# A hybrid decoder step with streamed expert rows: ring of eight, three weight places, reworked first attention and new order tables

## The chip, the cores and the metric

The kernel runs on one core of a Trainium2 chip. The metric is the device time of one launch in microseconds. The kernel before took 2222.21 us (median of 3 runs, 2209.38 to 2229.83). The engines are TensorE (PE), VectorE (DVE), ScalarE (ACT), GpSimd (POOL) and SyncE (SP), and 16 DMA engines that SP's and POOL's queues feed.

## What is computed

One inference step for 256 prompt tokens (tiles A and B, 128 tokens each) and 8 sample tokens (tile S), two layers, all in float32, D = 1024. Every sub-layer is RMS-normed and modulated (shift, scale, gate) by a vector from `silu(c) @ w_mod + b_mod`. Layer 0 mixes tokens by latent attention (the samples over 2048 cached positions), layer 1 by a gated MLP (SGU) with causal 128x128 mixing. Each is followed by PEER, which fetches 16 experts for each of 8 heads of each token:

```python
q = (xt @ w_q).reshape(PEER_BLOCK, PEER_HEADS, 2, PEER_HALF)
s1 = jnp.einsum('thk,nk->thn', q[:, :, 0], sub_keys[0])
s2 = jnp.einsum('thk,nk->thn', q[:, :, 1], sub_keys[1])
t1, i1 = lax.top_k(s1, PEER_TOPK)
t2, i2 = lax.top_k(s2, PEER_TOPK)
cand = (t1[..., :, None] + t2[..., None, :])   # 16 x 16, of which again the top 16
idx = e1 * N_KEYS + e2
g = jax.nn.softmax(top, axis=-1)
act = jax.nn.gelu(jnp.einsum('thkd,td->thk', u_tab[idx], xt))
out = jnp.einsum('thk,thkd->td', g * act, v_tab[idx])
```

## The kernel before

**Tiling and stages.** `schedule()` writes the program as a list of stages, which all engines walk in the same order: init, modulation chunks (`mod`), norm, `mla_in`, `attn`, `tables` (transposed keys), `proj`, norm, then `query` and one `route` for each head; after this come tile B, the samples and their eight `cache` stages, the SGU stages of layer 1 (`sgu_v`, `sgu_u`, `sgu_mix`, `sgu_out`), and the sample chain at the end (`proj`, `query_s`, `topk_s`, 16 `sgu_s`, `sgu_out`, `query_s`, `topk_s`). An engine signals each finished piece of a stage by one semaphore count, and others wait for the count (`after`, `begin`).

**The stream.** A *slot* is one expert index of one head: a gather of 128 rows of peer_u (1024 floats each) into `uring` and one of peer_v into `vring`. There are 512 slots for the prompt and 16 for the samples. POOL issues the gathers (`gather`, L779) in the order of the string PLAN_POOL: U and V, with K and C for cache pages. It waits for the indices of the head (DVE's "topk") and, from slot 7 on, for the slot's place in the ring to be free. DVE takes a U row (`dot`, L1932), 16 dots are put through a gelu in `gelu` (P) and `weights` (W), ACT makes a scaled diagonal from each weight (`diagonal`, L1453), and PE adds the V row, times that diagonal, to `yacc` (`value_sum`, L1217). A U row's place is free after the dot, a V row's after PE. When all slots of a tile are summed, DVE copies `yacc` out (`drain`, Y).

**Order.** The stream is woven into the stages by tables. At every signal, link and point an engine calls `spot()`; PLAN_PE, PLAN_DVE and PLAN_ACT say at which count how many units of the stream follow (V on PE; U, P, W, Y on DVE; D, T on ACT). PLAN_SP says the same for weight chunks on SP.

**Weights.** They come in chunks of 0.75 to 1 MB (`load_chunk`, L673). After the first query chunk they go through `wring`, four places; before it, while the rings are unused, uring and vring give six more places (`AHEAD`). A place is loaded again when PE has used its chunk. `EARLY` puts modulation chunks 8 to 19 inside `mla_in` and `attn` of tile A: 2 and 2, then 4 and 4.

**Steps that the change touches.** `rsqrt` (L1515 to L1521) is a chain of 14 small DVE instructions, each waiting for the one before. `norm` takes its square sum on DVE (L1524), then makes h in two passes over 1024 columns. `attn` goes through two halves of four heads, one after the other, in one set of buffers. `gate_row` and `residual` copy a row block from PSUM on DVE (L1678, L1670). `pick` (L1706 to L1733) finds the experts of one head; its last signal, "topk", releases the gathers.

Of the kernel before, what the change touches and what calls it, by code (L numbers as in the profile page):

```python
# [16 lines left out]
U32 = mybir.dt.uint32  # L17
# [28 lines left out]
RING = 7  # L46
WRING = 4
# [64 lines left out]
189:VVVVVVVVVVVVVVVV 197:VVV 199:V 200:VVVVV 207:V 208:VVVVVV 213:VVV 217:VV 218:V 232:V 237:VV 239:V 260:VV 280:V  # L112
285:V 290:VV 295:V 300:VVVVVVVVV 320:VVVVVVVVVVVVVVVVVVVVVVVVVV 323:VVVVV 331:VVV 334:VVVV 339:VVVVV 342:VVVV 358:V
361:VVVVVVVV 363:VV 364:VV 369:V 379:V 382:VV 383:V 397:VVVVVVVV 399:V 400:VVVV 405:V 417:VVVVVVVVVV 422:VV 426:VVV
428:V 460:VVV 503:VVV 508:VVVV 529:VVV 534:VVVV 557:VV 565:VV 567:VVV 569:VVVVVVVVVVVVV 581:VV 582:VV 595:V
596:VVVVVVVVVV 598:V 599:V 604:VV 629:VV 631:VV 639:VVVV 640:V 650:V 654:VVVVVVVVV 656:V 657:VV 662:V
676:VVVVVVVVVVVVVVV 677:V 688:V 691:VVVVVVVVV 693:V 694:VV 699:V 703:VVVVV 707:VVV 709:V 741:VVV 784:VVV 789:VVVV
810:VVV 815:VVVV 838:VV 840:VVVVVVVVVVVVVVVVVVVVV 854:V 855:VV 869:VVVVVVVV 871:V 872:VV 877:V 902:VV 904:VV 912:VVV
913:V 919:V 923:V 927:VVVVVVVVV 929:V 930:VVV 935:V 949:VVVVVVVVVVVVVVVVVVV 950:V 964:VVVVVVVV 966:V 967:VV 972:VV
976:V 985:VV 990:VVVVV 993:VV 1000:VV 1002:VV 1004:VV 1006:VV 1008:VV 1012:V 1013:VVVV 1019:VVVVVVVVVVVVVVVVV  # L120
1025:VV 1027:V 1039:VV 1042:V 1048:V 1054:V 1060:V 1066:V 1072:V 1075:VV 1079:VVVVV 1081:V 1090:VVV 1092:V 1094:V
1102:VV 1109:V 1111:V 1113:V 1115:V 1117:V 1121:V
1122:VVVVVVVVVVVVVVVVVVVVVVVVVVVVVVVVVVVVVVVVVVVVVVVVVVVVVVVVVVVVVVVVV 1128:VVVVVV
"""
PLAN_ACT = """
121:T 127:DDDDDDDDDDDDDDDD 145:TDDDDDDDDDD 147:D 148:D 149:DDDD 158:TDDDDDDDDDD 162:DDDTDDD 173:D 179:DD 181:TDD
186:DDD 190:DDD 196:DDDD 208:DD 210:DDDDD 215:DDD 219:DDDDDDD 229:TDDDDDDDDDDDDDDDD 242:T 243:DDDDDDDDDDDDDDDD 252:T
263:T 264:D 267:DDDDDDDDDD 269:DD 270:DD 283:DD 284:D 298:TDDDDDDDDDD 300:DDDDDDDDDDTDDDDDDDDD 318:D 335:DDD 338:T
356:DDD 359:DDDDDDDDDDD 373:T 379:DD 381:DDDDD 394:DD 398:DDDDD 402:DDDD 406:DD 407:DD 408:TDD 421:D
422:DDDDDDDDDDDD 425:TDD 436:DD 438:DDDDD 447:D 448:D 458:TD 462:DDDDDDDDDD 464:DD 465:DDDDDD 470:DDTDDD 474:DDDD  # L130
482:D 483:D 494:D 497:DDDDTDDDDDD 499:DDDDDDDDDDD 507:DT 524:DDD 545:DDD 548:DDDDTDDDDDDD 568:DD 570:DDDDD 575:DD
579:DDDDDDDD 583:DDDDD 587:D 588:TD 589:DD 603:DDDDDTDDDD 605:DD 606:D 617:DD 619:DDDDD 629:D 630:T 635:D 639:DT
643:DDDDDDDDDD 645:DDD 646:DDDD 651:DDDDDDDDDD 655:DDDD 663:DD 664:D 666:T 678:DDDDDDDDD 680:DDTDDDDDDDDDD 695:DDDD
701:DDDDDDDD 708:D 709:D 713:DDDDTDDDDDDDTDDDDDDDTDDDD 722:DDDDD 739:DDDD 756:D 759:DDTDDDDDDDDDD 775:DDD 781:DDDDT
788:D 789:DDD 793:DDDDDDDDDDDTDDDDDDDDDDDDDDDDTDDDDDDDDTDDDDDDDDDDDDDDDDDDDDDDDDDD
"""
PLAN_DVE = """
210:U 224:U 252:U 266:U 287:U 301:UUUUUU 333:U 347:U 368:U 382:U 401:U 402:P 403:UW 417:U 437:U 438:U 452:U 476:U
# [28 lines left out]
VVVVVVVVVVVVVVVVVVVVVVVVVVVV  # L167
"""
PLAN_SP = """
1:WWWWWWWW 30:WWWWWWWWWWWW 34:WWWWWWWWWWWWWWWWWWWWWWWWWWWWWWWWW 124:WWWWWWWWWWWWWWWWWWWW 181:WWWWWWWW  # L170
224:WWWWWWWWWWWWWWWWWWWWWWWWWWWWWWWWWW 341:WWWWWWWWWWWW 367:WWWWWWWWWWWWWWWWWWWWWWWWWWWWWW 458:WWWWWWWWWWWWWWWW
516:WWWWWWWWWW
"""
# [1844 lines left out]
```

## Time and profile before

| what | us |
|---|---|
| median of 3 runs | 2222.21 |
| lowest, highest | 2209.38, 2229.83 |
| span of the profiled execution | 2207.0 |
| PE, DVE, POOL, ACT busy | 1531.2, 1395.3, 1212.1, 355.5 |
| first gather issued at | 163.35 |

The profiled execution is known by its span alone, from its first to its last instruction; it lies 15.2 us below the median. Busy shares are means over stages of very different kinds, so the windows (busy time of each engine in a stretch, with the granted TensorE clock as a share of 2.4 GHz, the busy share of the DMA engines, which by its counting can pass 1, and GB/s) say more than the page. In the timeline a row is one instruction, or several alike, with the time that its engine was idle before and what ended that.

### The profile page before, as it was taken

To read this page: it belongs to the slowest core of one execution; us is meant where nothing else is said; L and a number is where in the kernel's file an instruction comes from. 1 tells how busy PE (TensorE), PEld (TensorE's weight loads), DVE (VectorE), ACT (ScalarE), POOL (GpSimd) and SP (SyncE) were. 2 spreads that over 40 slices of the span, in tenths; PEclk is the share of its full clock that TensorE was granted. 3 is DMA by queue.
4 is the path that set the end of the run, shared out by engine and by line. 5 is a ranking of instruction groups with operands and counts; after the bars stand their busy time and mean duration, and the time that the engine had idled before them with its cause. 6 is when DMAs were issued, how large, how long until landed. Compare 5 with 4: busy or idle time off the path is not lost. (4 is left out here: it accounts for less than half of the span.)

```text
span 2207.0 us, 25764 instructions
## 1 busy us (share of the span) xinstructions
PE 1531.2 (69%) x9198; PEld 745.6 (34%) x9198; DVE 1395.3 (63%) x3469; ACT 355.5 (16%) x901; POOL 1212.1 (55%) x1097
## 2 busy tenths in 40 slices
PE   5676446865546879977687889968778850555567
PEld 2345113541123426533532437525423310111112
DVE  1447988599875655558498836499687327443641
ACT  0100112111112211013131201122223110111111
POOL 0004377545777574437475754467675438745774
PEclk8687778987877979888796888977887785578658
DMA  9719899998989899898798998989998889999998
GB/s 366 276 47 403 291 374 335 413 362 329 384 323 370 297 417 419 341 364 315 274 347 316 315 362 345 377 324 338 363 339 302 323 317 338 380 419 419 335 350 310
DMA packets 213942, 751.57 MB, mean 341 GB/s; under 512 B 27236, under 2 KB 35628, under 8 KB 213816
## 3 DMA queue, kind: packets, MB, share of 16 engines
q0 software_dynamic: 155136, 564.20, 68.4%
q1 hardware_dynamic: 58680, 185.72, 21.6%
q8 instruction: 74, 1.21, 0.2%
q14 instruction: 52, 0.43, 0.1%
HBM read 747.74 MB, written 2.10 MB: 340 GB/s over the span
## 5 line engine op out<-in xcount | busy, mean ns | idle before, releaser
L779 POOL DMA_INDIRECT uring<-in_peer_u,expert x512 | 580.6, 1134 | 511.5 <-DVE dots L1932 211.0
L1217 PE MATMUL yacc<-vring,diag 64*64 64x512 f32 x4096 | 653.6, 738 | 229.9 <-DMA vring<-in_peer_v,expert 163.2
L779 POOL DMA_INDIRECT vring<-in_peer_v,expert x512 | 556.4, 1087 | 425.8 <-PE yacc L1217 290.4
L1932 DVE CUSTOM_DVE_ANT_0 uring<-uring,h 128x1024 f32<-128x1024 f32 x512 | 615.3, 1225 | 161.4 <-DMA uring<-in_peer_u,expert 144.1
L1217 PEld LDWEIGHTS yacc<-vring,diag 64*64 64x64 f32 x4096 | 155.2, 156 | 610.0 <-DMA vring<-in_peer_v,expert 338.8
L1453 ACT ACTIVATE diag<-cst,wts 128x64 f32<-128x64 f32 (+1 forms) x528 | 172.9, 344 | 868.7 <-PE yacc L1217 630.0
L1005 PE MATMUL pp<-hT,wring 128*128 128x128 f32 x992 | 132.3, 294 | 21.7 <-issue 15.9
L1005 PEld LDWEIGHTS pp<-hT,wring 128*128 128x128 f32 x992 | 125.8, 208 | 35.4 <-issue 29.6
L1805 DVE TENSOR_REDUCE arena<-arena 128x16 f32<-128x1024 f32 x64 | 77.8, 1215 | 28.6 <-ACT arena L1392 27.7
L1706 DVE MAX8 t<-sc 128x8 f32<-128x128 f32 (+1 forms) x68 | 19.9, 292 | 117.5 <-ACT sc L1253 83.2
L1068 PE MATMUL pq<-w_uk,arena 128*128 128x512 f32 x128 | 74.6, 672 | 22.9 <-ACT arena L1392 22.9
L836 PE MATMUL ps<-cst,arena 128*128 128x128 f32 (+2 forms) x101 | 22.2, 368 | 90.8 <-issue 29.0
L1068 PE MATMUL pp<-w_uk,arena 128*128 128x512 f32 x128 | 75.2, 677 | 2.7 <-ACT arena L1392 2.6
L1069 PEld LDWEIGHTS ps<-qabs,arena 128*128 128x128 f32 x256 | 51.7, 202 | 67.7 <-issue 67.7
L989 PE MATMUL pq<-vring,diag 128*32 128x256 f32 x128 | 12.8, 510 | 73.4 <-DMA vring<-in_peer_v,expert_s 72.0
L989 PE MATMUL ps<-wring,hTs 128*32 128x256 f32 (+1 forms) x384 | 39.2, 534 | 33.9 <-DMA wring<-in_peer_w_q 16.2
L979 PE MATMUL pp<-wring,arena 128*128 128x512 f32 x136 | 60.8, 603 | 0.7 <-DMA wring<-in_sg_w_out 0.7
L1253 ACT ACTIVATE arena<-ps 128x512 f32<-128x512 f32 (+6 forms) x75 | 38.6, 530 | 139.5 <-PE pq L1132 50.0
L868 PE MATMUL pq<-wring,siluT 128*32 128x256 f32 x448 | 36.8, 489 | 26.7 <-DVE mrows L1555 25.3
L836 PEld LDWEIGHTS ps<-cst,arena 128*128 128x128 f32 (+2 forms) x101 | 15.4, 187 | 112.4 <-issue 72.5
L1855 DVE TENSOR_TENSOR arena<-arena 128x1536 f32<-128x1536 f32 (+1 forms) x6 | 8.2, 1363 | 67.6 <-ACT arena L1253 49.6
L899 PE MATMUL ps<-mrows,cst 128*128 128x256 f32 x128 | 39.2, 460 | 6.1 <-issue 6.1
(301 smaller groups left out, 1854.0 us busy)
## 6 DMA issues: line engine op xcount, KB each, us to landing
wring<-in_peer_w_q SPq DMA_DIRECT2D x47, 1024.0 KB
wring<-in_w_mod SPq DMA_DIRECT2D x38, 1024.0 KB
wring<-in_sg_w_in SPq DMA_DIRECT2D x48, 768.0 KB
wring<-in_sg_w_out SPq DMA_DIRECT2D x18, 1024.0 KB
wring<-in_mla_w_o SPq DMA_DIRECT2D x9, 1024.0 KB
uring<-in_peer_u,expert POOLq DMA_INDIRECT x512
vring<-in_peer_v,expert POOLq DMA_INDIRECT x512
uring<-in_w_mod SPq DMA_DIRECT2D x6, 1024.0 KB, 16.7
```

The costliest lines, as they stand in the source:

```text
L779: pool.indirect_dma_start(ring[:, slot % RING, :], None, table[n // 3], bass.IndirectOffsetOnAxis(ap=idx, axis=0)).then_inc(land[slot % RI ...
L899: last = pe.matmul(out[:, q // 2, 256 * (q % 2):256 * (q % 2) + 256], ident[:, one:one + 1].to_broadcast([P, P]), mrows[:, r, :], start=Tr ...
L979: last = pe.matmul(pp[:, q], lhs[:, P * g:P * g + P], w[:, c, 512 * q:512 * q + 512], start=g == 0, stop=g == 2 * n - 1)
L989: last = pe.matmul(out[32 * q:32 * q + 32, 0:n], lhs, w[:, n * q:n * q + n], start=first, stop=final)
L1005: last = pe.matmul(pp[:, j // 4, P * (j % 4):P * (j % 4) + P], w[:, c, P * j:P * j + P], hT[:, kk, :], start=kk == 0 and j % 4 == 0, stop= ...
L1068: pe.matmul(kn_bank[j % 2][:, i], lhs, w_uk[:, :], start=True, stop=True)
L1069: last = pe.matmul(ps[0][:, H * tile:H * tile + H], lhs, qabs[:, b, :], start=False, stop=True, skip_group_check=True)
L1217: last = pe.matmul(yacc[64 * q:64 * q + 64, r], diag[at, slot % RING, :], v[at, 512 * q:512 * q + 512], start=first, stop=final)
L1253: return act.activation(out, in_, ACT.Copy)
L1453: act.activation(diag[:, slot % RING, 0:base.shape[-1]], base, ACT.Copy, scale=wts[:, p % 2, slot - SLOT0[p]:slot - SLOT0[p] + 1]).then_in ...
L1805: signal(dve.tensor_reduce(ssn[:, 16 * j:16 * j + 16], knsq[:, 1024 * (j % 2):1024 * (j % 2) + 1024].rearrange("p (i d) -> p i d", d=NOPE) ...
L1932: dve.tensor_tensor_reduce(u, u, rows_h[:, :], 1.0, 0.0, ALU.mult, ALU.add, dots[:, p % 2, i:i + 1]).then_inc(u_used, 1)
```

## The change

The rings of gathered rows have eight places in place of seven, and `wring` three in place of four; the early part so has eight places in the rings (`AHEAD`). Modulation chunks 20 to 23 of layer 0 move from after the first queries into the stages before the attention, and `tables` moves ahead of the attention, with its copies on ACT. The first tile's attention is `attn_alone`, which keeps both halves in flight in separate buffers. The square sum of prompt norms, the gate-row copies, the drains and half of the last attention copy move from DVE to ACT; `rsqrt`, the gelu polynomial and `pick` have fewer instructions; a new signal "expert" releases the gathers. All five order tables are new: of PLAN_PE and PLAN_SP a row stands here, since the others tell a reader as little.

```diff
-RING = 7
-WRING = 4
+RING = 8
+WRING = 3
 PLAN_PE = """
-189:VVVVVVVVVVVVVVVV 197:VVV 199:V 200:VVVVV 207:V 208:VVVVVV 213:VVV 217:VV 218:V 232:V 237:VV 239:V 260:VV 280:V
+170:VVVVVVVVVV 179:V 181:VVVV 186:V 189:VV 190:V 191:V 192:V 193:VVVVV 201:VV 205:VVVVVV 206:V 209:VV 210:V 224:VVV
...
-_early = mods(0, 8, 20)
-for _s, _n in ((("norm", A, 0, 0), (0, 0)), (("mla_in", A), (0, 2, 2)), (("attn", A), (4, 4, 0))):
+_early = mods(0, 8, 24)
+for _s, _n in ((("norm", A, 0, 0), (0, 0)), (("mla_in", A), (0, 4, 8)), (("attn", A), (4, 0, 0))):
...
@@ POOL, gather @@
-                    after(pool, DVE, WHERE[("route", n, h)], "topk")
+                    after(pool, DVE, WHERE[("route", n, h)], "expert")
...
@@ PE @@
+            def attn_alone(k):
+                after(pe, DVE, k, "qT1")
+                after(pe, ACTE, k, "kT1")
+                for f in range(2):
+                    for i in range(4):
+                        h = 4 * f + i
+                        last = pe.matmul(pp[:, f, P * i:P * i + P], qT[0:QK, P * h:P * h + P],
+                                         kT[A][0:QK, P * h:P * h + P], start=True, stop=True)
+                    signal(last, f"s{f}")
+                point(k, 0)
+                for f in range(2):
+                    after(pe, DVE, k, f"p{f}")
+                    signal(transposes(ps[f], [prob[:, 512 * f + P * i:512 * f + P * i + P] for i in range(4)], P), f"pT{f}0")
+                for f in range(2):
+                    after(pe, ACTE, k, f"pT{f}0")
+                    signal(pe.matmul(pq[:, f], ckv[A][:, :], att[:, 512 * f:512 * f + 512], start=True, stop=True), f"ol{f}")
...
@@ ACT @@
             def norm(k, tile, layer, second):
...
+                    signal(act.activation(h_tok[tile][:, :], x[tile][:, :], ACT.Square, accum_out=scr[:, 0:1]), "sq")
...
+            def gate_row(k, tile, name):
+                after(act, PE, k, name)
+                signal(copy(h_tok[tile][:, :], pss[:, :, :].rearrange("p q n -> p (q n)")), "row")
...
+            def drain(i):
+                n = DRAINED[i]
+                act.wait_ge(v_used, last_slot(n))
+                copy(h_tok[n % 3][:, :], yacc[:, :, :].rearrange("p q n -> p (q n)")).then_inc(drained, 1)
...
@@ DVE, rsqrt, norm and pick @@
                 for _ in range(3):
                     link(tt(tmp, out, out, ALU.mult))
-                    link(tt(tmp, tmp, v, ALU.mult))
-                    link(ts(tmp, tmp, -0.5, 1.5, ALU.mult, ALU.add))
-                    link(tt(out, out, tmp, ALU.mult))
+                    link(stt(tmp, tmp, -0.5, v, ALU.mult, ALU.mult))
+                    link(stt(out, tmp, 1.5, out, ALU.add, ALU.mult))
...
-                link(stt(h, xr, scr[:, 1:2], gain, ALU.mult, ALU.mult))
-                signal(tt(h, h, shift, ALU.add), "h")
+                for q in range(1 if tile == S else 2):
+                    at = slice(0, QUAD) if tile == S else slice(512 * q, 512 * q + 512)
+                    link(stt(h[:, at], xr[:, at], scr[:, 1:2], gain[:, at], ALU.mult, ALU.mult))
+                    signal(tt(h[:, at], h[:, at], shift[:, at], ALU.add), "h" if tile == S else f"h{q}")
...
-                link(cp(cf[0:r, 0:2, :], cu[0:r, :, :]))
-                link(cp(cf[0:r, 2:4, :], ti[0:r, :, :]))
-                for i in range(2):
-                    hr = hot[0:r, :, :]
-                    link(tt(hr, over(cf[0:r, i, :], TOPK), times(const("iota16", r), TOPK), ALU.is_equal))
-                    link(tt(hr, hr, times(cf[0:r, 2 + i, :], TOPK), ALU.mult))
-                    link(dve.tensor_reduce(ef[0:r, i, :], hr, X, ALU.add))
-                link(stt(expert_out, ef[0:r, 0, :], float(NKEYS), ef[0:r, 1, :], ALU.mult, ALU.add))
+                link(cp(cf[0:r, :, :], picks[0:r, :, :]))
+                hr, h3 = hot[0:r, :, :, :], hot[0:r, :, :, :].rearrange("p i a b -> p (i a) b")
+                link(tt(h3, over(cf[0:r, 0:2, :].rearrange("p i a -> p (i a)"), TOPK), times(const("iota16", r), 2 * TOPK),
+                        ALU.is_equal))
+                link(tt(hr, hr, cf[0:r, 2:4, :].unsqueeze(2).to_broadcast([r, 2, TOPK, TOPK]), ALU.mult))
+                link(dve.tensor_reduce(ef[0:r, :, :].rearrange("p i a -> p (i a)"), h3, X, ALU.add))
+                signal(stt(expert_out, ef[0:r, 0, :], float(NKEYS), ef[0:r, 1, :], ALU.mult, ALU.add), "expert")
```

How the order moves. On PE in the head, from the end of `mla_in` (the 512-wide matmul into ps) to `proj` (`pp<-wring,arena 128x512`). A modulation chunk is 8 matmuls `siluT`, the table transposes are those of `diag` and `w_uk`. Before:

```order
L926 MATMUL ps<-w_uk,arena 128x512
L868 MATMUL yacc<-wring,siluT 32x256 x24
L868 MATMUL yacc<-uring,siluT 32x256 x8
L836 MATMUL ps<-cst,arena 96x128 x8
L836 MATMUL pq<-cst,arena 96x128 x8
L947 MATMUL pp<-arena 128x128 x4
L868 MATMUL yacc<-uring,siluT 32x256 x16
L868 MATMUL yacc<-vring,siluT 32x256 x16
L836 MATMUL ps<-cst,arena 128x128 x4
...
L961 MATMUL ps<-arena,w_uv 128x128 x8
L836 MATMUL ps<-cst,diag 128x128 x4
L836 MATMUL pp<-cst,w_uk 128x128 x4
```

With the change:

```order
L943 MATMUL ps<-w_uk,arena 128x512
L885 MATMUL yacc<-wring,siluT 32x256 x24
L885 MATMUL yacc<-uring,siluT 32x256 x32
L885 MATMUL yacc<-vring,siluT 32x256 x32
L885 MATMUL yacc<-wring,siluT 32x256 x8
L853 MATMUL ps<-cst,diag 128x128 x4
L853 MATMUL pp<-cst,w_uk 128x128 x4
L853 MATMUL ps<-cst,arena 96x128 x8
L853 MATMUL pq<-cst,arena 96x128 x8
L993 MATMUL pp<-arena 128x128 x8
L885 MATMUL yacc<-wring,siluT 32x256 x16
L982 MATMUL ps<-arena,w_uv 128x128 x8
```

Twelve modulation chunks and the table transposes stand ahead of the attention's own transposes in place of four chunks, and all eight score matmuls stand together.

On PE at tile B's `sgu_out` (its matmuls are `pp<-wring,arena 128x512`, 24 calls; a slot of the stream is four calls of `yacc<-vring,diag`). Before:

```order
L1217 MATMUL yacc<-vring,diag 64x512 x16
L899 MATMUL ps<-mrows,cst 128x256 x4
L979 MATMUL pp<-wring,arena 128x512 x24
L1217 MATMUL yacc<-vring,diag 64x512 x12
L899 MATMUL pp<-mrows,cst 128x256 x4
```

With the change:

```order
L1257 MATMUL yacc<-vring,diag 64x512 x12
L916 MATMUL ps<-mrows,cst 128x256 x4
L1019 MATMUL pp<-wring,arena 128x512 x4
L1257 MATMUL yacc<-vring,diag 64x512 x4
L1019 MATMUL pp<-wring,arena 128x512 x8
L1257 MATMUL yacc<-vring,diag 64x512 x4
L1019 MATMUL pp<-wring,arena 128x512 x4
L1257 MATMUL yacc<-vring,diag 64x512 x4
L1019 MATMUL pp<-wring,arena 128x512 x8
L1257 MATMUL yacc<-vring,diag 64x512 x8
L916 MATMUL pp<-mrows,cst 128x256 x4
```

Three slots now stand inside the projection, which had none. In tile A's the 24 calls stay together.

## Rows read from the trace of the kernel before

**Rows 1.** The page: span, busy us (share) xinstructions by engine, bytes from HBM.
```profile
span 2207.0 us, 25764 instructions
...
PE 1531.2 (69%) x9198; PEld 745.6 (34%) x9198; DVE 1395.3 (63%) x3469; ACT 355.5 (16%) x901; POOL 1212.1 (55%) x1097
...
HBM read 747.74 MB, written 2.10 MB: 340 GB/s over the span
```

**Rows 2.** Windows: stretch, length, busy us (x) by engine, PEclk, DMA share, GB/s.
```profile
0.00:163.00 163.00, 100.24 (x609) 61.10 (x613) 56.58 (x158) 15.96 (x38) 1.73 (x9) 0.79 0.62 231
...
163.00:2180.00 2017.00, 1414.47 (x8469) 678.72 (x8461) 1332.95 (x3306) 336.99 (x854) 1201.77 (x1079) 0.79 0.93 350
```

**Rows 3.** Windows of 20 us and one of 100 us in the stream.
```profile
840.00:860.00 20.00, 20.00 (x145) 14.81 (x144) 12.42 (x24) 3.99 (x7) 7.83 (x5) 1.00 1.02 416
...
1060.00:1080.00 20.00, 17.95 (x105) 14.31 (x102) 17.82 (x53) 2.84 (x9) 7.61 (x8) 0.68 0.49 163
...
1800.00:1820.00 20.00, 10.68 (x77) 3.45 (x75) 4.91 (x5) 0.35 (x1) 6.13 (x6) 0.76 0.47 143
...
2080.00:2180.00 100.00, 70.47 (x344) 13.94 (x344) 31.39 (x62) 14.24 (x44) 73.14 (x69) 0.64 0.96 352
```

**Rows 4.** POOL's waits, whole span: total us, times, longest us.
```profile
POOL vring L779 <- PE yacc L1217: 290.7, 126, 16.2
...
POOL uring L779 <- DVE dots L1932: 211.0, 68, 9.2
```

**Rows 5.** Timeline, tile B's SGU and samples: start, us, instruction [idle <-releaser].
```profile
1355.76 2.18 POOL L779 DMA_INDIRECT vring<-in_peer_v,expert  x1 [0.30 <-issue]
...
1370.97 0.94 POOL L779 DMA_INDIRECT vring<-in_peer_v,expert  x1 [13.02 <-PE yacc L1217]
...
1376.37 17.33 PE L979 MATMUL pp<-wring,arena 128*128 128x512 f32 x40
...
1399.72 1.50 POOL L779 DMA_INDIRECT vring<-in_peer_v,expert  x1 [11.89 <-PE yacc L1217]
...
1813.48 0.94 POOL L779 DMA_INDIRECT uring<-in_peer_u,expert_s  x1 [7.80 <-DMA gate_s<-route_g]
```

**Rows 6.** Timeline of the head, up to the first gather.
```profile
35.24 0.16 DVE L1518 TENSOR_TENSOR rs<-scr 128x1 f32<-128x1 f32 x1
...
81.87 1.91 PE L836 MATMUL ps<-cst,arena 128*96 128x128 f32 x8 [11.38 <-issue]
...
97.56 0.69 DVE L1649 TENSOR_TENSOR arena<-pp,cst 128x512 f32<-128x512 f32 x1 [0.19 <-PE pp L947]
...
99.21 0.40 ACT L1305 ACTIVATE arena<-arena,scr 128x128 f32<-128x128 f32 x1 [3.81 <-DVE scr L1651]
...
106.46 0.69 DVE L1658 COPY arena<-pq 128x512 f32<-128x512 f32 x1 [3.58 <-PE pq L957]
...
112.38 0.63 PE L836 MATMUL ps<-cst,diag 128*128 128x128 f32 x4 [1.63 <-issue]
...
114.66 3.75 PE L899 MATMUL ps<-mrows,cst 128*128 128x256 f32 x8 [1.22 <-issue]
...
141.60 1.22 DVE L1573 TENSOR_TENSOR h<-h,ps 128x1024 f32<-128x1024 f32 x1
...
160.14 0.43 DVE L1728 TENSOR_TENSOR hot<-hot,cf 128x256 f32<-128x256 f32 x1
...
163.35 1.08 POOL L779 DMA_INDIRECT uring<-in_peer_u,expert  x1 [161.08 <-DVE gate L1733]
```

**Rows 7.** The chain of waits in the sample tail: start, us, what.
```profile
1766.61 15.97 DMA wring<-in_peer_w_q
...
2004.02 18.20 DMA wring<-in_peer_w_q
```

**Rows 8.** Tile wring: what PE idled for before reading it: us, times.
```profile
  DMA wring<-in_peer_w_q: 45.2, 23
...
  DMA wring<-in_sg_w_in: 17.5, 15
```

More of the change, by code:

```diff
@@ L229, in schedule @@
     first = heads(A, (1, 1, 2, 4))
-    start = ([("init",)] + mods(0, 0, 8) + [("norm", A, 0, 0), ("mla_in", A), ("attn", A), ("tables",), ("proj", A),
+    start = ([("init",)] + mods(0, 0, 8) + [("norm", A, 0, 0), ("mla_in", A), ("tables",), ("attn", A), ("proj", A),
                                             ("norm", A, 0, 1)] + first[:2])
@@ L313, in labels @@
     if kind == "route":
-        return [], ["top", "topk"], ["exp"]
+        return [], ["top", "expert", "topk"], ["exp"]
     if kind == "query_s":
@@ L317, in labels @@
     if kind == "topk_s":
-        return [], ["top", "topk"], ["exp"]
+        return [], ["top", "expert", "topk"], ["exp"]
     if kind == "sgu_init":
@@ L936, in attn @@
                         signal(transposes(out, [q3[:, i, h, :] for h in range(4 * f, 4 * f + 4)], P), names[f])
-                for f in range(2):
+                if tile == A:
+                    attn_alone(k)
+                for f in range(2 * (tile != A)):
                     if f == 0:
@@ L958, in attn @@
                     signal(last, f"ol{f}")
-                after(pe, DVE, k, "ol1")
+                after(pe, DVE, k, "ol0" if tile == A else "ol1")
+                if tile == A:
+                    after(pe, ACTE, k, "ol1")
                 for h in range(H):
@@ L1300, in attn @@
                     signal(copy(kT[tile][0:QK, 512 * f:512 * f + 512], pq[0:QK, f]), f"kT{f}")
-                for f in range(2):
+                if tile == A:
+                    attn_alone(k)
+                for f in range(2 * (tile != A)):
                     after(act, DVE, k, f"max{f}")
@@ L1640, in attn @@
                     signal(cp(qT[0:QK, 512 * f:512 * f + 512], ps[f][0:QK, :]), f"qT{f}")
-                for f in range(2):
+                if tile == A:
+                    attn_alone(k)
+                for f in range(2 * (tile != A)):
                     after(dve, PE, k, f"s{f}")
@@ L1958, in point @@
                 spot()
[L1960 removed]
+            stages = dict(init=init, mod=mod, norm=norm, mla_in=mla_in, attn=attn, proj=proj, route=route, topk_s=topk_s,
                           cache_init=cache_init, cache=cache, cache_out=cache_out, sgu_init=sgu_init,
```

240 lines of the change are left out of this document (144 added, 96 removed).

## The prediction

> **What bounds the kernel now.** I read the page first: no compute engine is busy for more than 69% of the span of 2207.0 us, while the DMA engines move 747.74 MB from HBM, a mean of 340 GB/s [rows 1]. The bytes don't change with this edit: 1024 gathers of expert rows (128 rows of 4 KB, 0.52 MB each), 32 for the samples, and the weights. So I cut the span where the stream of gathers begins and ends [rows 2]. In the first 163 us the DMA engines are 0.62 busy at 231 GB/s, since nothing can be gathered before the first head's experts are known; from 163 to 2180 us they are 0.93 busy at 350 GB/s; a tail of 27 us is left. 350 GB/s x 2017 us is 706 MB. The kernel ends when these 706 MB have passed, so two things count: when the first gather starts, and how much of the stream's time the DMA engines are without work.
>
> What takes their work away is seen in slices of 20 us [rows 3]: 416 GB/s where weights and gathers both flow (840 to 860), but 163 GB/s at 1060 and 143 at 1800, the two deepest of many such holes. The waits of POOL, which issues the gathers in one fixed order, say why [rows 4]: 290.7 us for PE to free a V row, 211.0 us for DVE to free a U row. The piece at 1360 us shows the form [rows 5]: POOL stands 13.02 us until PE, done with the mixing of an SGU tile, takes V rows again, and 11.89 us more during the output projection. Near 1813 it waits 7.80 us for the samples' route to come back from DRAM. POOL is in order, so a V gather that waits holds the U gathers behind it.
>
> **The change part by part.** The sum is made against the span of 2207.0 us; the median of the runs is 2222.2, 15.2 more, and I add that at the end.
>
> *The head, up to the first gather at 163.35 us [rows 6].*
> - rsqrt goes from 14 to 8 chained instructions. One takes 0.16 us (at 35.24) and some 0.03 to the next. Three such chains lie on the path (two in mla_in, one in the second norm), 6 x 0.19 = 1.15 us each: 3.5. That of the first norm is hidden, as the rows from PE come later.
> - The norm's output in two halves lets PE start on the first while DVE makes the second. The add takes 1.22 us (141.60); half of it and of the multiply are covered, less one more issue: 0.9 per norm, two norms, 1.8. The square sum, a pass of the same length, goes from DVE to ACT, which must wait for x as well: between 0.3 lost and as much won, I take 0.
> - First attention: today half 1 starts its mask at 97.56 and ends its last copy at 107.15 (106.46 + 0.69), after half 0. With scores, maxima, exponents and transposes of both halves in flight at once, all but the slowest stage of that chain of 9.6 us goes. The exponents of one half are four instructions of 0.4 (1.6 us), and 0.7 comes from splitting the last copy between DVE and ACT: 9.6 - 1.6 + 0.7 = 8.7. Bounds: 4 if PE waits for weights in between, and 11, since eight modulation chunks lay inside this stage before and four do now.
> - The key tables stood alone between 112.38 and 114.66; they now lie under DVE's work before the attention, where PE idles: 2.3. If that cover is gone it costs the same again.
> - Top-k: two casts become one, and twice three instructions of 0.43 (160.14) become three of twice the size, 0.7 each; the gather waits for the experts and no longer for the gate, which ended two instructions later: 0.2 + 0.5 + 0.4 = 1.1.
>
> Together 17.4. PE now does twelve modulation chunks before the attention in place of four; today it stands idle for 11.38 us there (81.87), and eight more of about 0.9 us fit in. If they land late, up to 5 of the gain is lost. **Head: -17.**
>
> *Four more weight chunks before the first gather.* The last four modulation chunks of layer 0 (4 x 1.05 MB) move out of the stream into the head, where the DMA engines are 0.38 idle. At 416 GB/s [rows 3] that is 10.1 us of stream. With three places for weights in place of four one chunk fewer lies ready when the gathers start: 2.5 back. Their row's four bias loads of some 0.3 us of issue each now stand ahead of w_o on SP's queue, which idles there. **-7.6.**
>
> *Eight ring slots and the new order.* A ring of seven rows is 7 x 0.52 MB = 3.7 MB, 8.8 us at 416 GB/s; eight rows give 1.3 us more in each ring before POOL must stop. PE's new order puts V rows into long pieces that had none: tile B's output projection was 24 calls of two passes, 0.43 us each (17.33 us for 40, [rows 5]), 21 us without a V row, and is now cut into pieces of 4 to 8 calls; in tile A it stays whole, and one V stands in the mixing. DVE sheds about 90 us of its 1395.3 [rows 1]: 34 top-k picks x 0.6, twelve copies of a row block and eight square sums x 1.23 to ACT, 29 rsqrt x 6 x 0.2, and the gelu polynomials. That eases the 211.0 us behind DVE. ACT takes some 25 us on top of 355.5; queued behind its new waits are diagonals for PE, and they waited for PE anyway. The bounds of all this: nothing, if other waits take the place of these, or the whole of the idle share. From 0.93 to 0.99, a little below the 1.02 of the slice at 840, is 2017 x 0.06 = 122 us. By the two orders and such durations, what PE's pieces without a V row have beyond 9 us (a ring's worth) falls from some 270 to some 125 us in all, about half. So I take half: **-61**.
>
> A smaller effect has only a far row. Issuing a gather takes 0.94 us when undisturbed but 2.18 us at 1355.76, while DVE runs a 1536-wide multiply [rows 5]. Fewer DVE passes mean fewer long issues; POOL has spare time in most slices, so between 0 and 10 us, and I take 0. [...]
>
> Sum: 2207.0 - 17 - 7.6 - 61 = 2121.4, plus 15.2: **2137**.
>
> **Rivals.**
> 1. *The stream runs at the memory's rate, not at its idle share.* For it: from 2080 to 2180 us almost only gathers flow, the DMA engines are 0.96 busy, and yet they move 352 GB/s [rows 3], no more than the mean of the whole stream. Then more slots only make packets wait longer, and the stream gains at most from 350 to 352, 0 to 11 us: 2207 - 24.6 - 6 + 15.2 = 2192. Against it: slices at 416. The Trainium skill (DMA: Bandwidth & Descriptors, "Where 436 GB/s comes from") puts the HBM side of one core at about 358 GB/s and says that this side binds; by it the stream's floor is 706 / 0.358 = 1972 us, a gain of at most 45, and the time 2153. The slices at 416 GB/s contradict it as a ceiling. Chance 0.18.
> 2. *Nearly all holes close* (share 0.99): -122 in place of -61, 2075. Against it: tile A's projection is as long as before, and the samples' route through DRAM [rows 5] stays. Chance 0.17.
> 3. *Slower: three places for weights starve PE.* In the sample tail PE waits for chunk after chunk, 15.97 and 18.20 us for one [rows 7], while the gathers share the queues. At 18.2 us from issue to landing, four places give PE a chunk each 4.55 us, three one each 6.07, 1.5 us more. Before the two kinds of chunk with the most transfers PE idles in 38 places already [rows 8], and there nothing hides the 1.5: 57 us, during which no V row is freed. If this takes the place of the stream's gain, the end is 2207 - 24.6 + 57 + 15.2 = 2255. It decides from the point where chunks are used faster than one each 6 us while the queues are full. Against it: those 38 waits are only 62.7 us today, short next to the landing time, and a queue asked for fewer chunks lands each sooner. Chance 0.07.
> 4. *The new order does not do what it says*, and leaves waits of the same size at other places, with the head's gain alone: 2198 to 2205. It is the upper edge of my forecast's own range; chance 0.06.
>
> **How the numbers follow.** The forecast has the remaining 0.52, with 2075 to 2190 as its own range. The likeliest time is 2137. For 8 in 10, I reach down to 2070 and up to 2200: this leaves out rival 3, half of rival 4, and the lower half of rival 2. A change of 1% is 22 us, about what a measurement of this kernel can tell from none. Faster by more (below 2200): 0.52 + 0.17 + 0.12 of rival 1 + 0.02 = 0.83. Within 1%: 0.10. Slower: 0.07.
>
> **What the profile after would show.** First U gather at 144 to 149 us in place of 163.35, with no table copies between attention and projection. The stretch from there to the tail at 0.95 to 0.97 DMA share and 358 to 368 GB/s. POOL's waits for PE down to 150 to 200 us, for DVE to 130 to 180, DVE busy near 1305. In the sample chain, chunk waits of 15 to 20 us each. I would be wrong if the first gather comes at 155 or later (weights land late), if the share rises and the rate doesn't (rival 1), or if the chain of waits in the last 400 us is a row of weight chunks with POOL idle behind the route (rival 3).

## The result, and the profile after

The changed kernel took 2257.7 us (median of 4 runs, 2254.28 to 2264.02) beside 2221.55 for the kernel before on the same chip: a ratio of 1.0202, 95% interval [1.0158, 1.0245]. It is 2% slower; 2137 was predicted, and "faster" had 0.83.

The page of the profile after: span, busy us by engine, bytes.

```profile
span 2256.8 us, 25572 instructions
...
PE 1575.3 (70%) x9198; PEld 777.6 (34%) x9198; DVE 1321.2 (59%) x3189; ACT 349.1 (15%) x934; POOL 1200.9 (53%) x1097
...
HBM read 747.74 MB, written 2.10 MB: 332 GB/s over the span
```

DVE sheds 74.1 us against [rows 1] and the bytes are the same, but the span is 49.8 us longer. The medians are 36.2 us apart: the execution profiled before is the fastest of its kernel, the one profiled here is an average one, so some 14 us of what the two traces show between them is no effect of the change. The windows of the change, with the columns of [rows 2]:

```profile
0.00:140.00 140.00, 93.96 (x661) 56.14 (x665) 48.15 (x135) 21.61 (x47) 1.73 (x9) 0.88 0.76 292
...
140.00:2230.00 2090.00, 1465.80 (x8405) 716.37 (x8401) 1269.77 (x3051) 322.77 (x874) 1188.35 (x1077) 0.78 0.90 336
...
900.00:920.00 20.00, 19.65 (x87) 12.97 (x86) 5.27 (x3) 3.77 (x7) 1.05 (x2) 0.62 0.45 168
1060.00:1080.00 20.00, 20.00 (x116) 9.39 (x118) 14.38 (x20) 8.77 (x17) 16.04 (x14) 1.00 0.84 285
1100.00:1120.00 20.00, 20.00 (x118) 14.39 (x119) 16.81 (x49) 1.88 (x6) 6.61 (x7) 0.67 0.31 86
...
2080.00:2180.00 100.00, 68.15 (x436) 21.17 (x436) 49.53 (x118) 10.19 (x41) 61.45 (x56) 0.75 0.99 385
```

The head is shorter and fuller, as hoped (292 GB/s up to 140 us in place of 231 up to 163). The stream after it went the wrong way: the share fell from 0.93 to 0.90 and the rate from 350 to 336 GB/s over a stretch of 2090 us in place of 2017. The hole at 1060 closed (163 to 285 GB/s), a deeper one opened at 1100 (86).

Since the bytes are the same, the two traces can be laid side by side by the bytes moved. The change is ahead by 34 us when 40 MB are in, by 15 at 205 MB, level at 235, behind by 4 at 265, by 49 at 325, 35 at 445, 59 at 565 and 53 at 745 MB. So 45 us go in 60 MB, over half of the 87 us between the lead of 34 and the lag of 53. (The first 14 us of the lead go between 40 and 100 MB, where POOL waits 26.76 and 14.76 us for dots, at 206 and 222 us below.) These two windows, before and after, hold just those 60 MB, tile A's gated MLP and its output projection:

```profile
814.00:968.00 154.00, 146.67 (x870) 88.36 (x870) 77.42 (x149) 20.28 (x45) 71.95 (x61) 0.93 0.97 389
```

```profile
818.00:1017.00 199.00, 160.67 (x854) 95.70 (x846) 74.91 (x149) 21.53 (x52) 69.71 (x65) 0.85 0.82 300
```

The first answers with 389 GB/s, the second with 300. The timeline of the change shows who stood still in it (start, us, instruction, idle before and its releaser), with the first gather at its head:

```profile
140.50 1.08 POOL L796 DMA_INDIRECT uring<-in_peer_u,expert  x1 [138.24 <-DVE expert L1830]
...
206.23 0.94 POOL L796 DMA_INDIRECT uring<-in_peer_u,expert  x1 [26.76 <-DVE dots L2022]
221.92 0.94 POOL L796 DMA_INDIRECT uring<-in_peer_u,expert  x1 [14.76 <-DVE dots L2022]
...
871.42 0.93 POOL L796 DMA_INDIRECT vring<-in_peer_v,expert  x1 [19.67 <-PE yacc L1257]
...
905.99 0.94 POOL L796 DMA_INDIRECT vring<-in_peer_v,expert  x1 [12.47 <-PE yacc L1257]
...
919.89 0.94 POOL L796 DMA_INDIRECT vring<-in_peer_v,expert  x1 [12.96 <-PE yacc L1257]
...
934.36 10.57 PE L1019 MATMUL pp<-wring,arena 128*128 128x512 f32 x24
...
952.34 12.37 PE L1019 MATMUL pp<-wring,arena 128*128 128x512 f32 x24 [7.42 <-DMA wring<-in_sg_w_out]
...
964.75 1.22 DVE L1780 TENSOR_TENSOR h<-h,pp 128x1024 f32<-128x1024 f32 x1 [34.52 <-PE pp L1019]
...
967.26 1.22 DVE L2022 CUSTOM_DVE_ANT_0 uring<-uring,h 128x1024 f32<-128x1024 f32 x1
...
968.76 0.93 POOL L796 DMA_INDIRECT uring<-in_peer_u,expert  x1 [25.21 <-DVE dots L2022]
```

Read it backwards from the last row. POOL waits 25.21 us for a dot; the dot stands on DVE behind the residual, which waits 34.52 us for the projection; and the projection, one run of PE work without a V row, waits 7.42 us in its middle for a weight chunk. Ahead of it POOL had waited 19.67, 12.47 and 12.96 us for V rows. The waits over the whole span (us, times, longest):

```profile
POOL vring L796 <- PE yacc L1257: 342.7, 91, 19.7
POOL uring L796 <- DVE dots L2022: 179.7, 34, 26.8
PE yacc L1257 <- ACT diag L1542: 115.4, 12, 33.4
DVE h L1780 <- PE pp L1019: 67.5, 3, 34.5
```

Against [rows 4], POOL's waits for PE grew by 52.0 us and those for DVE shrank by 31.3; both are fewer and longer, up to 26.8 us where 9.2 was the longest for DVE. PE now waits 115.4 us for ACT's diagonals; the row before was

```profile
PE yacc L1217 <- ACT diag L1453: 26.0, 2, 13.9
```

What PE idled for before reading a weight place, to be held against [rows 8]:

```profile
  DMA wring<-in_peer_w_q: 66.1, 26
  DMA wring<-in_sg_w_out: 43.1, 12
  DMA wring<-in_sg_w_in: 39.2, 23
```

w_q grew from 45.2 to 66.1 us, sg_w_in from 17.5 to 39.2. The kind that grew most is not in [rows 8]; before, it was

```profile
  DMA wring<-in_sg_w_out: 17.7, 8
```

With w_mod (14.2 to 33.2) and w_o (15.7 now) the waits for weights went from some 95 to some 197 us.

### The profile page after: what moved, and what is told of

Same layout as the page of the kernel before. It is cut to its first block, busy times and chain, and to the rows that moved or that the text cites. A ratio compares the mean times of both kernels' runs of the same rounds, so it can differ in the third digit from the quotient of the medians.

```text
span 2256.8 us, 25572 instructions
## 1 busy us (share of the span) xinstructions
PE 1575.3 (70%) x9198; PEld 777.6 (34%) x9198; DVE 1321.2 (59%) x3189; ACT 349.1 (15%) x934; POOL 1200.9 (53%) x1097
## 4 chain that ended last, share of the span: by engine, by line
PE 24%; DMA 12%; DVE 11%; issue 11%; POOL 6%; another core or an unknown queue 5%; ACT 2%; SPq 1%; POOLq 0%; DVEq 0%; ACTq 0%
PE yacc L1257 6%; POOL uring L796 4%; DVE uring L2022 3%; DMA wring<-in_sg_w_in 3%; DMA vring<-in_peer_v,expert 2%; PE pp L1108 2%; POOL vring L796 2%; PE pp L1019 2%; PE pq L1108 2%; PE ps L1143 2%; DMA uring<-in_peer_u,expert 1%; DMA wring<-in_peer_w_q 1%; PE pp L1045 1%; DMA wring<-in_sg_w_out 1%
## 5 line engine op out<-in xcount | busy, mean ns | idle before, releaser
L1257 PE MATMUL yacc<-vring,diag 64*64 64x512 f32 x4096 | 671.1, 730 | 241.7 <-ACT diag L1542 115.4
L796 POOL DMA_INDIRECT uring<-in_peer_u,expert x512 | 576.2, 1125 | 470.0 <-DVE dots L2022 179.7
L796 POOL DMA_INDIRECT vring<-in_peer_v,expert x512 | 550.4, 1075 | 503.4 <-PE yacc L1257 341.0
L1257 PEld LDWEIGHTS yacc<-vring,diag 64*64 64x64 f32 x4096 | 172.2, 156 | 603.9 <-issue 445.1
L1542 ACT ACTIVATE diag<-cst,wts 128x64 f32<-128x64 f32 (+1 forms) x528 | 149.0, 337 | 327.7 <-PE yacc L1257 180.2
L1780 DVE TENSOR_TENSOR h<-h,pp 128x1024 f32<-128x1024 f32 x8 | 9.8, 1220 | 124.4 <-PE pp L1019 67.5
L853 PE MATMUL ps<-cst,h 128*128 128x128 f32 x72 | 16.5, 362 | 50.5 <-DVE h L1662 48.4
L1428 ACT ACTIVATE eg<-ctop,eg 128x16 f32<-128x16 f32 (+1 forms) x34 | 10.4, 305 | 266.2 <-DVE eg L1820 152.9
L1143 PEld LDWEIGHTS ps<-arena,kv 128*128 128x128 f32 x256 | 49.3, 297 | 5.6 <-issue 5.6
L1143 PE MATMUL ps<-arena,kv 128*128 128x8 f32 x256 | 50.0, 335 | 0.0
```

The source lines that it names most:

```text
L796: pool.indirect_dma_start(ring[:, slot % RING, :], None, table[n // 3], bass.IndirectOffsetOnAxis(ap=idx, axis=0)).then_inc(land[slot % RI ...
L1143: pe.matmul(ps[1][:, 264:272], kv[:, i, :], pr[:, H * i:H * i + H], start=i == 0, stop=False)
L1257: last = pe.matmul(yacc[64 * q:64 * q + 64, r], diag[at, slot % RING, :], v[at, 512 * q:512 * q + 512], start=first, stop=final)
L1542: act.activation(diag[:, slot % RING, 0:base.shape[-1]], base, ACT.Copy, scale=wts[:, p % 2, slot - SLOT0[p]:slot - SLOT0[p] + 1]).then_in ...
```

## The experiments

Each run has the kernel before beside it on the same chip, and only ratios to that are compared, since the kernel before took 2211.86 us in the first set of four runs, 2087.88, 2085.49 and 2087.27 in the next three, and 2188.9 in the last, of two. "7/4" is seven ring rows and four weight places, "8/3" the sizes of the change. The three parts of the change are its *sizes*, its *code* (head, DVE chains, copies on ACT) and its *tables*.

### Sizes

**e1: the change with the old sizes.** Two tables had to be adapted for it in one place each: in PE's, four V rows stand up to ten spots earlier, in ACT's, one diagonal stands two later. POOL's string is the change's, letter for letter; the move in it that the expectation names was not made.

```diff
-RING = 8
-WRING = 3
+RING = 7
+WRING = 4
```

> The changed kernel with the two sizes set back: seven rows in each ring and four weight places, all its tables kept but for two places where eight rows were needed (one V and the diagonal behind it move by a few spots, and two V gathers stand one later in POOL's string). My theory, that the new tables and not the sizes cost the time (the bytes lag by 20 us less than before at 205 MB and by 49 us more at 325 MB, with POOL behind PE and DVE): 2245 to 2280 us, no gain over 2258. The rival that three weight places starve PE: 2200 to 2228. The rival that eight rows are worth a lot and only hide the fault: 2285 or more.

Measured: 1.0146 [1.0063, 1.023], 2240.2 us, between the theory and the first rival. With the change's own tables the trade of sizes is worth 0.6% by the medians, inside the intervals. By the bytes e1 loses the same 35 us between 265 and 325 MB, so that hole belongs to code and tables; from there it goes back to 19 us behind at 745 MB, while the change stays at 53 (e1's profiled execution is its fastest, 15 us below its median).

The 0.6% is not the price of a weight place. PE's idle time before weight places fell from some 197 to 84 us, of which these are two kinds:

```profile
  DMA wring<-in_peer_w_q: 43.3, 13
  DMA wring<-in_sg_w_out: 8.3, 2
```

But tables made for eight rows don't suit seven: POOL now stands longer in the first hole, where the change waits 26.76 and 14.76 us, for a V row that PE has not taken yet:

```profile
230.64 0.93 POOL L796 DMA_INDIRECT vring<-in_peer_v,expert  x1 [51.94 <-PE yacc L1257]
```

**e2: the kernel before with the new sizes**, and a table of SP in which eight of the 183 weight loads are issued at a later spot, one of them in the line shown.

```diff
-RING = 7
-WRING = 4
+RING = 8
+WRING = 3
 PLAN_SP = """
-1:WWWWWWWW 30:WWWWWWWWWWWW 34: ...
+1:WWWWWWWW 30:WWWWWWWWWWW 34: ...
```

> The kernel before with eight rows in each ring and three weight places and nothing else, but that each weight chunk from the thirteenth on is loaded one place of SP's table later, as three places need it. Theory (sizes are nearly neutral): 2205 to 2240 us against 2222. If three places starve PE: 2255 to 2280. If eight rows help the stream by themselves, as the prediction had it: 2200 or less.

Measured: 1.0447 [1.0348, 1.0545], 96 us over and beyond the range of each rival. By the bytes it is 11 us behind at 265 MB and 99 at 745; 27 us of that fall into the same 60 MB, the rest comes bit by bit.

**e5: only one weight place fewer (7/3)**, with e2's table of loads, and **e18: that table alone (7/4)**, its control.

```diff
-WRING = 4
+WRING = 3
```

> The kernel before with three weight places and its seven rows, tables as in the run of it with eight and three. That run took 4.5% more than before, and PE waited some 120 us for weights in place of some 45. If the third weight place taken away is the cause: 2285 to 2325 us again. If eight rows with tables made for seven are: 2205 to 2235.

> A control for the runs of the kernel before with three weight places, which also had each load from the thirteenth on one place later in SP's table: here that table with all four places and seven rows. If the lost place made their 3.9 and 4.5%: within 1% of before. If the later loads did: 1.02 or more.

Measured: e5 1.0385 [1.0318, 1.0451], e18 0.9999 [0.9966, 1.0032]. The order of loads costs nothing that shows, so the fourth place is worth 3.9% of the kernel before. What PE idled for before reading a weight place, in e18 and then in e5:

```profile
  DMA wring<-in_peer_w_q: 44.5, 22
  DMA wring<-in_sg_w_in: 36.3, 23
```

```profile
  DMA wring<-in_peer_w_q: 114.8, 38
  DMA wring<-in_sg_w_in: 56.2, 34
```

For w_q, 16 more waits and 70.3 us more. Over all kinds these waits grew by some 170 us, of which only 30 lie in the sample tail after 1740 us. Set against e2 (of another set), the eighth ring row bought nothing in the old order.

**e12, e6, e7: one set of tables (e4's, below) at 7/4, 7/3 and 8/3.** Only the two sizes differ.

> The changed code with the tables by the rule, seven rows and four places, on the chip of the last three. It took 0.981 of before on a chip with slow gathers; the same tables took 1.018 with seven rows and three places and 1.010 with eight and three on a chip with fast ones. If the fourth place is what separates them, 0.97 to 0.99 here. If chips and not places did: 1.00 or more.

> The changed code with the tables of the run with seven rows and four places (2171 us), letter for letter, and three weight places. If the fourth place is worth what separated the two new plans (2218 against 2171): 2205 to 2230 us. If that gap came from the eight rows or from chance in the tables: 2165 to 2185.

> The same tables again with eight rows and three places, the sizes of the change. Beside the run with seven and three it shows what the eighth row is worth: if nothing, within 10 us of it; by the prediction's reasoning (1.3 us more in each ring at many of the waits), 15 to 40 us less. Against 2171 it shows the trade as a whole: slower if weight places are worth more than rows.

Measured: 7/4 0.9966 [0.9931, 1.0001] (2078.86 us), 7/3 1.018 [1.011, 1.025] (2127.85), 8/3 1.0104 [1.0039, 1.017] (2110.53). The kernel before took 2085.49 and 2087.88 us beside them, so the times compare: the fourth weight place is worth 49 us, the eighth ring row 17 by the medians (the two intervals overlap), and the trade of one for the other costs 32. The 0.9966 of 7/4 met neither of its two expectations: the advantage of 1.9% that these tables had in the first set was not there again. PE's idle time before weight places, at 7/4 and then at 7/3:

```profile
  DMA wring<-in_peer_w_q: 52.6, 24
  DMA wring<-in_w_mod: 27.6, 14
```

```profile
  DMA wring<-in_peer_w_q: 91.4, 33
  DMA wring<-in_w_mod: 80.9, 25
```

### Code

**e13: the kernel before with the shorter DVE chains alone** (rsqrt, gelu, picks), every unit of the stream at its old neighbour.

```diff
-                    link(tt(tmp, tmp, v, ALU.mult))
-                    link(ts(tmp, tmp, -0.5, 1.5, ALU.mult, ALU.add))
-                    link(tt(out, out, tmp, ALU.mult))
+                    link(stt(tmp, tmp, -0.5, v, ALU.mult, ALU.mult))
+                    link(stt(out, tmp, 1.5, out, ALU.add, ALU.mult))
+                    spot()
```

> The kernel before with one part of the change alone: the shorter DVE chains (rsqrt 14 to 8 instructions, gelu polynomial 3 to 2, the merged top-k casts and one-hot passes). Every place of every table and both sizes stay as they were. DVE's share of the prediction's stream term by itself. If the chains ease POOL's waits for dots as the prediction had it: 10 to 35 us less than before. If DVE's work was under other waits and its spare time only becomes more waiting: within 10 us of before.

Measured: 0.9915 [0.9883, 0.9947], some 18 us, as the first expectation had it. DVE is busy for 1348.1 us, 47 of the 74 us that the change sheds.

**e17: e13 with the head** (attention with both halves in flight, key tables ahead of it on ACT, all 16 early modulation chunks ahead of it), 7/4, old tables.

```diff
-_early = mods(0, 8, 20)
-for _s, _n in ((("norm", A, 0, 0), (0, 0)), (("mla_in", A), (0, 2, 2)), (("attn", A), (4, 4, 0))):
+_early = mods(0, 8, 24)
+for _s, _n in ((("norm", A, 0, 0), (0, 0)), (("mla_in", A), (0, 4, 8)), (("attn", A), (4, 0, 0))):
```

> The kernel before with two parts of the change: the shorter DVE chains (alone 0.9915 of before) and the head (first attention with both halves in flight, tables copied by ACT ahead of it, sixteen modulation chunks before it and none woven into the first heads). Seven rows and four places, every V, dot, diagonal and POOL's string as before; copies and drain stay on DVE. If the head's 20 us and more are kept where the tables are left alone: 0.975 to 0.987, faster than both kernels. If an earlier first gather is given back whatever the order, as it was in the change by 235 MB: 0.988 to 0.995.

Measured: 0.9862 [0.98, 0.9924], faster than the kernel before and, by its ratio, than the change. POOL's waits in e18 (the kernel before in the same set) and in e17:

```profile
POOL vring L779 <- PE yacc L1217: 307.0, 119, 18.1
POOL uring L779 <- DVE dots L1932: 194.8, 70, 9.2
POOL uring L779 <- DVE gate L1733: 160.8, 1, 160.8
```

```profile
POOL vring L785 <- PE yacc L1246: 299.6, 127, 15.5
POOL uring L785 <- DVE dots L2005: 176.5, 62, 10.8
POOL uring L785 <- DVE gate L1805: 140.8, 1, 140.8
```

The gathers start 20 us earlier, and by the bytes e17 is 32 us ahead at 40 MB and 46 ahead at 745. By the medians it is 31 us ahead. That these two parts lose nothing is shown. How much of the head's 20 us is kept is not: the chains alone gave 0.9915, so the head adds 0.5%, some 12 us, inside the intervals and between two sets. Nor does e17 clear all of the code. It has the square sums, copies and drains on DVE, h in one piece and the gathers behind "topk", so what eats the lead in the change is order, size or one of these.

### Tables

**e3 and e4: the changed code with tables written by one rule** (each unit at the spot where an estimate of the engines' progress has its rows landed), at 8/3 and at 7/4.

```diff
 PLAN_PE = """
-170:VVVVVVVVVV 179:V 181:VVVV 186:V 189:VV ...
+181:VVVVVVVVVVVVVVVV 190:VVV 191:V 195:VVVV 196:VV ...
```

> The changed kernel with its code and sizes untouched, but the four tables of PE, ACT, DVE and POOL written anew by one rule: an engine takes a V, U, diagonal or polynomial only where its rows are in and its own next step has to wait, or from near the place of the old table on; POOL issues whatever has a free row. Theory (the order is the fault): the holes at 640 to 740 and 820 to 1020 us go, 2170 to 2225 us. If the order is not at fault but the sizes, or ACT's added copies, or the memory's rate: 2240 to 2275.

> The same code of the changed kernel and the same rule for the tables, with seven rows and four weight places. Theory: 2160 to 2215 us, some 0 to 20 us less than with eight and three, since a wait for weights holds PE's own chain and a ring of seven rows already lasts as long as most pieces without a V. If eight rows are the better size: 15 us or more slower than the run with eight and three. If the order is not at fault: 2240 or more.

Measured: e3 1.0007 [0.9961, 1.0053], e4 0.9808 [0.9732, 0.9884] (e12, the same kernel in another set, 0.9966: the gain over the kernel before depends on the set). With other tables, the change's code and sizes (and its table for SP) lose their 2% in this set (e3), and with the old sizes on top the kernel is faster than the one before in one set and even in the other. In the faster sets the same steps are 1.0216 for the change (e9, below), 1.0104 with e4's tables at 8/3 (e7) and 0.9966 at 7/4 (e12): tables 1.1%, sizes 1.4%. So both are at fault, and their shares depend on the path. Both come out of the first 310 MB 6 or 7 us ahead, where the change is 40 behind.

**e8: the changed code at 7/4, its units on PE, DVE and ACT back at their old neighbours**, within two spots.

```diff
 PLAN_PE = """
-170:VVVVVVVVVV 179:V 181:VVVV 186:V 189:VV ...
+181:VVVVVVVVVVVVVVVV 190:VVV 191:V 195:VVVVV 199:V ...
```

> The changed code (head, first attention, shorter DVE chains, copies on ACT) with seven rows and four places and with PE's, DVE's and ACT's units at the places of the kernel before, stage by stage, within two spots; POOL issues as rows come free. What the code alone is worth: the head's 23 us and some of DVE's 90 us: 2170 to 2205 us if the theory holds that code is good and tables and sizes are at fault. 2215 or more if the code's gain is lost whatever the order.

Measured: 1.0293 [1.0216, 1.0369], no better than the change, and a miss for the theory that its code is good. POOL's order had been rewritten with it, so this does not give the value of the old tables in the new code. It leaves open whether POOL's order or the part of the code that e17 lacks makes the 4% between the two.

**e11: the kernel before under e4's rule**, 7/4 (its diff is of the same kind).

> The code and the sizes of the kernel before (7 and 4) with tables written by the same rule as in the run of the changed code with seven and four that took 0.981 of before. It tells what the code of the change is worth when neither side has the advantage of its tables. If the code gains (head 23 us, DVE 74 us lighter): this one 0.99 to 1.00 of before, and the next one 30 to 60 us below it. If all the gain was in the rule: this one near 0.98 as well.

Measured: 1.0585 [1.0513, 1.0656]. A miss for both expectations. The rule's tables cost the old code 5.9%, so a table has no worth apart from the code that it is for; between e11 and e12 the code is worth 6%, which says more of the fit of rule and code than of the code.

**e9: the change once more**, beside e10.

> The changed kernel as it is, beside the next three on one chip, since the kernel before took 2212 us on the chip of the first four runs and 2088 on that of the next four. Its ratio to before was 1.0202. If the loss goes with the order and the weight places: 1.01 to 1.035 on any chip. If it came from the slow gathers of one chip (350 to 365 GB/s in stretches of gathers alone there, 410 to 418 on the other): under 1.01 on a chip with the fast ones.

Measured: 1.0216 [1.0142, 1.0289], as the first time, though the kernel before took 6% less here: the loss does not hang on a slow set.

**e10, e14, e15: the change with units moved ahead.** In e10 188 of DVE's 596 units come earlier, in e14 99 V rows on PE, in e15 both (133 and 181). (In e10 six dots also stand later, by up to six spots.) From e10's table:

```diff
 PLAN_DVE = """
-... 216:U 283:U 324:U 338:U 343:U 346:U 348:P 352:WUU 361:U ...
+... 216:U 279:UUUUUPUU 352:W 361:U ...
```

> The changed kernel with one table edited, PLAN_DVE: 188 of its 596 units (168 dots, 12 P, 8 W) stand earlier, before steps at which DVE otherwise stands idle until PE or ACT is done (in the changed kernel it idles 34.5 us for PE at the residual of tile A's output projection while POOL waits 25.2 us for the dot behind it, and 26.8 us at 206 us). Nothing stands later, and the other tables and sizes are the change's. If DVE's in-order units are what makes the new holes: 20 to 45 us less than the changed kernel on this chip, and POOL's waits for dots of over 10 us nearly gone. If the holes only move to the V rows behind PE, or if the weight places set the end: within 10 us of it.

> The changed kernel with PLAN_PE alone edited: 99 of the 528 V products stand earlier, before steps at which PE otherwise idles; dots and the other tables as in the change. With 188 units of DVE earlier, POOL's waits for dots fell by 86 us and those for V rows rose by 122, and the time rose by 34 us. If V rows behind PE are what limits: 10 to 30 us less than the changed kernel (1.005 to 1.016 of before, where it took 1.0216). If a unit that stands too early only makes its engine wait for the row, whatever the engine: 0 to 35 us more.

> The changed kernel with V products (133) and DVE units (181) both earlier, the diagonals, POOL's string and the sizes as in the change. If the two have to move together, since a V row is free only after its dots, its diagonal and its product: 15 to 40 us less than the changed kernel, though either alone gives nothing. If earlier units cost as such: as much over the changed kernel as the dots alone or more, 1.035 to 1.05 of before.

Measured: e10 1.0386 [1.0312, 1.0459], e14 1.0228 [1.0178, 1.0278], e15 1.0316 [1.0257, 1.0375], against 1.0216 for e9. None gains; e10 is clearly slower, e14 level, e15 between them. The waits of e10, and then of e14:

```profile
POOL vring L795 <- PE yacc L1256: 438.2, 136, 26.9
DVE uring L2021 <- DMA uring<-in_peer_u,expert: 286.0, 137, 12.8
...
POOL uring L795 <- DVE dots L2021: 59.2, 24, 18.2
```

```profile
PEld yacc L1257 <- DMA vring<-in_peer_v,expert: 317.8, 162, 10.9
POOL vring L796 <- PE yacc L1257: 288.3, 131, 20.4
...
POOL uring L796 <- DVE dots L2022: 164.8, 52, 22.1
```

In e9, without the moves, POOL waits 144.7 us for dots and 315.9 for V, DVE 184.6 for U rows and PE's weight loads 235.0 for V rows. In e10 POOL's waits for dots fall to 59.2 us, and those for V rise to 438.2: DVE, in order, now stands for U rows that haven't landed (286.0 us), and its stage work, which PE waits for, comes late. In e14 PE's weight loads take the wait (317.8 us). DVE's units too early cost more than they had cost too late; PE's cost as much.

**e16: e4's tables with 35 V and 146 DVE units ahead.**

> The best version so far (changed code, tables by the rule, seven rows and four places: 0.981 and 0.997 of before on two chips) with 35 V products and 146 DVE units earlier by the same reasoning. If moving units ahead helps where both move: 0.97 to 0.99 of before. If not: 10 to 30 us over the version it comes from, 1.00 to 1.01.

Measured: 1.0149 [1.0105, 1.0193] against 0.9966 for e12: the same lesson, 1.8% lost from good tables.

## Why the prediction was wrong, by its own steps

**The head: right, a little small.** First gather at 140.50 us, predicted 144 to 149: 22.9 us earlier where I reckoned 17 (and 20 in e17). PE took all twelve chunks before the attention without a delay that shows: its waits for weights in the first 163 us are 9 us, as before (10).

**Four more chunks before the first gather, -7.6: right in kind.** Together the two terms promised 24.6; the change is 34 us ahead at 40 MB, and e17 32; but the change is only 20 ahead at 100 MB.

**"Eight ring slots and the new order", -61: the step that failed.** From the first gather on, the change takes 2256.8 - 140.5 = 2116.3 us where the kernel before took 2207.0 - 163.35 = 2043.7: 73 more (some 14 of them from the choice of the profiled execution), in place of 61 fewer beyond the 7.6. (2017 x 0.06, from which the 61 came, is 121 and not 122.) The term had these parts:

- *DVE's lighter load.* Nearly right in size: 74 us fewer where 90 were reckoned. The chains, 47 of these, give 0.9% alone (e13), a third of the 61.
- *The order.* I counted PE's pieces without a V row in two orders and read their halving as half of the idle share. That is a count of one engine. The waits are set by three in-order engines at once, and where tile A's projection, its residual, the dots behind it and late V rows come together, 45 us went in 60 MB. The expectation that POOL's waits would be 150 to 200 and 130 to 180 us met 342.7 and 179.7. The change at the old sizes stands at 1.0146 (e1), its chains and head with the old tables at 0.9862 (e17): 2.8% lie in the new tables and in the code that e17 lacks. That figure is rough: it stands between two sets, one kernel's ratio moved by 1.6% between sets (e4, e12), and e1 has the wait of 51.94 us.
- *ACT's new work, put at nothing because the diagonals "waited for PE anyway".* Before, they did: PE waited for them 26.0 us. With the change it waits 115.4. ACT's busy time did not rise by 25 us, it fell from 355.5 to 349.1, so it is not its load. Nor is it the copies as such: e3, e12 and e8 have them too, with 17.3, 30.7 and 29.3 us of this wait under other tables.
- *The eighth slot.* Worth 17 us by the medians under e4's tables (e6, e7), nothing that shows in the old order (e2, e5), and bought with a weight place.

**Three weight places.** The forecast took 2.5 us at the start of the stream; rival 3 had the mechanism, at 57 us and 0.07. The runs give 49 us (e6 against e12) and 80 (e5): the rival's mechanism and the order of its size were right, its chance was far too low. My argument against it, that 62.7 us of waits are short next to the landing time, was the wrong way round: short waits mean that four places just covered the landing time, and so that three don't. The other one, that a queue asked for fewer chunks lands each sooner, does not show: the median from issue to landing of a w_q chunk is 10.4 us with four places (e12) and 10.9 with three (e5, the other code). The 18.2 us that I took for it is the longest piece of a chain, and the place was off too: most of the growth lies in the prompt part and not in the sample tail, and sg_w_out, not among my 38 places, grew most in the change. Its point of decision, one chunk each 6 us, was not tested. In the change the whole trade of sizes is worth 0.6% by e1, although some 110 us of waits for weights go with it; the wait of 51.94 us hides a part, and that V rows late for other reasons leave time to load may be another, which no run shows. The rival's 2255 us agrees with the 2257.7 measured in part by chance: the hole between 265 and 325 MB stays at the old sizes.

**Rival 1, the memory's rate.** From 2080 to 2180 us the change moves 385 GB/s at a share of 0.99, against 352 at 0.96 [rows 3]: no ceiling at 352. Rival 4, an order that does not do what it says, was the nearest in kind; it stopped at no gain, and I gave no case in which a new order is worse than the old by itself. The issue time of gathers, bounded at 10 us and taken at 0: POOL's busy time fell by 11.2 us, from 1212.1 to 1200.9. In the sample chain, chunk waits of 15 to 20 us each were promised; this pair is what the chain of waits shows late in the change:

```profile
2075.07 10.52 DMA wring<-in_sg_w_out
...
2109.51 11.89 DMA wring<-in_peer_w_q
```

Shorter pieces than in [rows 7]. From 1740 to 2180 us PE idles some 90 us before weight places, where it was 71.

**What stays open.** PE's waits for diagonals, 115.4 us, are there in every kernel with the change's table for ACT (96.2 in e1 to 172.7 in e15), and 30.7 in e12 with another. No run changed that table alone, nor the copies on ACT alone, so how the 2.8% split between them was not tried. That the tables carry a large part follows from e3 and e4, which keep the code, copies and all, and are free of the loss in their set; against it stands e8, whose PE, DVE and ACT follow the old order and which is slow all the same. Why it is, no run shows.

## What to carry to other kernels

When a prefetch place is taken away, compare the landing time of a transfer over the number of places with the use of one, and do it for the busiest stretch: waits that are short today can be the edge and not a cushion. A hand-written order is right for one set of durations and sizes; judge a new one by the waits of all engines that it touches, since moving one engine's work ahead only moved the wait to the next here. And try the parts apart: here the chains and the head with the old tables were 1.4% faster, and the rest of the change turned that into 2% slower.

## What was not expected of the hardware

The kernel before took from 2085 to 2222 us in different sets of runs, a spread of 6.6%, while it agrees within 1% to 2% inside one. The changed kernel shows it too: 2257.7 us, and 2132.18 in e9. Its first 140 us run at 292 and 291 GB/s, so the difference lies in the stream: 336 GB/s at a share of 0.90 above, and in e9

```profile
140.00:2105.00 1965.00, 1385.71 (x8401) 678.28 (x8393) 1271.02 (x3051) 324.04 (x876) 1188.16 (x1077) 0.80 0.93 358
```

It is no lower top rate of the memory, since the slower set reaches it as well, here in the change:

```profile
2000.00:2025.00 25.00, 11.23 (x65) 1.88 (x64) 8.27 (x19) 1.76 (x7) 17.37 (x16) 0.59 1.02 421
```

The Trainium skill (DMA: Bandwidth & Descriptors, "Where 436 GB/s comes from") gives about 358 GB/s for the HBM side of one core; the 421 of this row and the 416 of [rows 3] don't agree with it as a ceiling. Why a set differs from another, no run here tells.
